# Second block's mixer: one written order of sixteen rounds for dilated attention and mLSTM, and six places for weights, in place of two generators taking turns

## The reference

```
def hybrid_mixer(h, w_in, gate_bias, g_q, g_k, g_mh, w_out):
    ...
    hm = bidirectional_mlstm(heads(mq, M_HEADS), heads(mk, M_HEADS) * (M_QK_DIM ** -0.5), heads(mv, M_HEADS),
                             gates[0], jax.nn.log_sigmoid(gates[1]), gates[2], jax.nn.log_sigmoid(gates[3]))
    hm = rms_norm(hm.transpose(0, 2, 1, 3), g_mh.reshape(M_HEADS, M_V_DIM))
    hm = (hm * jax.nn.sigmoid(mo.reshape(B, S, M_HEADS, M_V_DIM))).reshape(B, S, M_HEADS * M_V_DIM)
    ...
    ha = dilated_attention(qa, ka, heads(av, A_HEADS))
    ...
    return jnp.concatenate([hm, ha], axis=-1).astype(h.dtype) @ w_out
```

## Time and profile before

| what | value |
|---|---|
| median of 3 runs | 3207.26 us (3206.55 to 3207.32) |
| profiled execution | 3206.36 us, span 3204.4 us |
| PE busy | 3104.4 us (97% of the span) |
| DVE busy | 1905.7 us (59%) |
| ACT busy | 1042.2 us (33%) |
| POOL busy | 9.7 us |
| DMA | 369.19 MB, mean 115 GB/s |

### The profile page before, as it was taken

One profiled execution on the slowest core, in us unless ns is written; L12 is line 12 of the kernel. 1 busy time (PEld: TensorE's weight loads), 2 busy tenths in 40 slices (PEclk: granted clock), 3 DMA queues, 4 the chain that ended last, 5 costly groups with the idle time before them and its releaser, 6 DMA issues.

```text
span 3204.4 us, 37150 instructions
## 1 busy us (share of the span) xinstructions
PE 3104.4 (97%) x15012; PEld 2517.3 (79%) x15022; DVE 1905.7 (59%) x2786; ACT 1042.2 (33%) x1525; POOL 9.7 (0%) x23
## 2 busy tenths in 40 slices
PE   8999999998899999999999999999999998899998
PEld 7888888786678888788877888878887765578887
DVE  7876654636665555666657555466665565564434
ACT  4212222435442222422235222332223435442222
POOL 0000000000000000000000000000000000000000
PEclk9999999999999999999999999999999998899999
DMA  6433342210033443256532353235451220133231
GB/s 228 144 119 119 137 146 79 65 52 11 2 125 132 143 173 124 82 178 233 187 117 71 131 186 130 87 115 190 169 215 57 79 66 1 47 121 103 92 99 53
DMA packets 102964, 369.19 MB, mean 115 GB/s; under 512 B 11358, under 2 KB 12638, under 8 KB 102540
## 3 DMA queue, kind: packets, MB, share of 16 engines
q1 hardware_dynamic: 101788, 362.14, 33.2%
q0 software_dynamic: 1008, 4.69, 0.4%
HBM read 364.69 MB, written 2.10 MB: 114 GB/s over the span
## 4 chain that ended last, share of the span: by engine, by line
PE 86%; DVE 8%; ACT 4%; issue 1%; DMA 1%; SPq 0%; POOL 0%; DVEq 0%; ACTq 0%; POOLq 0%
PE ps L193 25%; PE ps L195 24%; PE ps L194 24%; PE ps L197 4%; PE ps L198 2%; DVE SQ L615 1%; DVE HL L604 1%; DVE WL L185 1%; PE ps L2869 1%; DVE XT L1038 1%; DVE RAW L1501 0%; DVE DUMP L306 0%; ACT WH L180 0%; DMA STG<-in_w_modt 0%; PE ps L500 0%
## 5 line engine op out<-in xcount | busy, mean ns | idle before, releaser
L193 PE MATMUL ps<-HH,WH 128*128 128x512 f32 x2400 | 947.2, 395 | 5.4 <-ACT S L915 2.2
L195 PE MATMUL ps<-HH,WL 128*128 128x512 f32 x2400 | 936.4, 390 | 0.0
L194 PE MATMUL ps<-HL,WH 128*128 128x512 f32 x2400 | 936.0, 390 | 0.0
L180 ACT ACTIVATE WH<-RAW 128x1024 fp32r<-128x1024 f32 x456 | 459.0, 1048 | 630.9 <-PE ps L195 361.8
L185 DVE TENSOR_TENSOR WL<-RAW,WH 128x1024 fp32r<-128x1024 f32 x456 | 542.7, 1219 | 75.3 <-ACT WH L180 75.1
L193 PEld LDWEIGHTS ps<-HH,WH 128*128 128x128 f32 x2400 | 450.9, 188 | 111.3 <-issue 10.2
L195 PEld LDWEIGHTS ps<-HH,WL 128*128 128x128 f32 x2400 | 450.9, 188 | 96.8
L194 PEld LDWEIGHTS ps<-HL,WH 128*128 128x128 f32 x2400 | 451.2, 188 | 95.7 <-issue 3.8
L1038 DVE SCALAR_TENSOR_TENSOR XT<-ps,DER,XT 128x512 f32<-128x512 f32 x512 | 346.6, 683 | 246.5 <-PE ps L195 231.7
L193 PE MATMUL ps<-GH,WH 128*128 128x512 f32 x1056 | 414.1, 392 | 4.8 <-DVE GL L946 4.8
L195 PE MATMUL ps<-GH,WL 128*128 128x512 f32 x1056 | 411.1, 389 | 0.0
(11 more groups left out here) (373 smaller groups left out, 2600.0 us busy)
## 6 DMA issues: line engine op xcount, KB each, us to landing
RAW<-in_w_modt SPq DMA_DIRECT2D x200, 512.0 KB, 5.0
RAW<-in_ffn_wi SPq DMA_DIRECT2D x182, 512.0 KB, 4.9
RAW<-in_w_gu SPq DMA_DIRECT2D x90, 512.0 KB, 4.5
RAW<-in_ffn_wo SPq DMA_DIRECT2D x88, 512.0 KB, 4.7
RAW<-in_w_in SPq DMA_DIRECT2D x44, 512.0 KB, 3.6
RAW<-in_w_down SPq DMA_DIRECT2D x44, 512.0 KB, 3.9
RAW<-in_w_out SPq DMA_DIRECT2D x16, 512.0 KB, 4.4
STG<-in_w_modt SPq DMA_DIRECT2D x10, 512.0 KB, 12.9
```

Source lines behind the costliest of these rows:

```text
L180: act.e.activation(u.hi, u.ld.view, ACT.Copy).then_inc(u.hi_done.sem, 1)
L193: pe.e.matmul(out, wh, x[0], start=first, stop=False)
L194: pe.e.matmul(out, wh, x[1], start=False, stop=False)
L195: m = pe.e.matmul(out, wl, x[0], start=False, stop=last)
```

## The change

`mlstm` and `dilated` are gone. One function, `rounds`, adds all their steps in one written order: for each r from 0 to 15 the attention pair r and the mLSTM unit r. `MlExp` is split into `MlWeights` (ScalarE) and `MlScore` (TensorE), so that they can stand apart. A has six places in place of four. `ptfree[3]` is not set any more, so all transposes go through bank 6. The weights of the output projection are split within the last steps.

```diff
-        self.afree = {s: NONE for s in range(4)}
+        self.afree = {s: NONE for s in range(6)}
...
-        self.A = sb("A", [128, 4, T])
+        self.A = sb("A", [128, 6, T])
...
-            s = m.na % 4
+            s = m.na % 6
...
-            self.side_by_side(self.mlstm(m, w, mix, a["w_out_2"]), self.dilated(w, mix))
+            self.rounds(m, w, mix, a["w_out_2"])
...
+        mixed = lambda k, ready: self.add(MixSplit(self, mix, [k], [ready]))
+        unit, last, den, quot, square, root, out = {}, {}, {}, {}, {}, {}, {}
+        split(0, True)
+        split(0, False)
+        self.add(MlMask(m, 0))
+        for r in range(16):
+            h, j = r // 4, r % 4
+            if r:
+                self.add(DilCount(w, r - 1))
+            unit[r] = self.add(MlWeights(m, h, j))
+            self.add(DilScore(w, r))
+            if r:
+                self.add(DilTrans(w, 2 * r - 2))
+            if h and j == 1:
+                quot[h - 1] = self.add(MlQuot(m, den[h - 1]))
+            self.add(MlScore(m, unit[r]))
+            if r:
+                self.add(DilTrans(w, 2 * r - 1))
+            if r == 1:
+                self.add(MlTurnFloor(m))
+            if h and j == 3:
+                out[h - 1] = self.add(MlOut(m, root[h - 1]))
+            if r > 1:
+                self.add(DilPV(w, r - 2))
+            if r:
+                last[r - 1] = self.add(MlSum(m, unit[r - 1]))
+            self.add(MlProd(m, unit[r]))
+            if h and j == 0:
+                den[h - 1] = self.add(MlDen(m, last[r - 1]))
+                self.add(DilDen(w, h - 1))
+            if h and j == 1:
+                square[h - 1] = self.add(MlSquare(m, quot[h - 1]))
+                self.add(DilQuot(w, h - 1))
+            if h and j == 2:
+                root[h - 1] = self.add(MlRoot(m, square[h - 1]))
+                mixed(3 + h, w.quot[h - 1].done)
+            if r in (2, 3):
+                split(1, r == 2)
+            if j == 3 and h < 3:
+                self.add(MlMask(m, h + 1))
+        self.add(DilCount(w, 15))
+        last[15] = self.add(MlSum(m, unit[15]))
+        self.add(DilTrans(w, 30))
+        den[3] = self.add(MlDen(m, last[15]))
+        self.add(DilTrans(w, 31))
+        self.add(DilPV(w, 14))
+        quot[3] = self.add(MlQuot(m, den[3]))
+        self.add(DilDen(w, 3))
+        self.add(DilPV(w, 15))
+        square[3] = self.add(MlSquare(m, quot[3]))
+        self.add(DilQuot(w, 3))
+        for k in range(2):
+            mixed(k, out[k].done)
+        root[3] = self.add(MlRoot(m, square[3]))
+        mixed(7, w.quot[3].done)
+        out[3] = self.add(MlOut(m, root[3]))
+        mixed(2, out[2].done)
+        mixed(3, out[3].done)
```

More of the change, by code:

```diff
@@ L2480, in vector @@
                                 m.MB[d * 4 + h].rearrange("p (n t) -> p n t", t=128), mk, ALU.add).then_inc(self.done[d].sem, 1)
-class MlExp(Step):
+class MlWeights(Step):
     def __init__(self, m, h, j):
@@ L2497, in __init__ @@
             self.off.append(m.P.s["ml_act"].next() if o.stop > o.start else self.diag[d])
-        self.qkfree = m.qkfree
-        self.qk = m.P.s["ml_mm"].next()
         m.unit[h, j] = self
@@ L2516, in scalar, with __init__ @@
                 act.e.activation(m.A[:, s, o], m.MB[d * 4 + h][:, o], ACT.Exp, bias=ub, scale=-1.0).then_inc(self.off[d].sem, 1)
+class MlScore(Step):
+    def __init__(self, m, x):
+        self.m, self.h, self.j = m, x.h, x.j
+        self.qkfree = m.qkfree
+        x.qk = m.P.s["ml_mm"].next()
+        self.done = x.qk
     def tensor(self, pe):
@@ L2527, in tensor @@
         pe.e.matmul(m.P.banks[0], m.KH[r, p, js], m.QL[r, p, :], start=False, stop=False)
-        pe.e.matmul(m.P.banks[0], m.KL[r, p, js], m.QH[r, p, :], start=False, stop=True).then_inc(self.qk.sem, 1)
+        pe.e.matmul(m.P.banks[0], m.KL[r, p, js], m.QH[r, p, :], start=False, stop=True).then_inc(self.done.sem, 1)
 class MlProd(Step):
@@ L3749, in mixer_hybrid, with rounds @@
         return [self.over]
-    def mlstm(self, m, w, mix, w_out):
+    def rounds(self, m, w, mix, w_out):
         m.qsplit, m.ksplit = {}, {}
[L3754 to L3759, removed]
-        self.add(MlFloor(m))
[L3761 to L3792, removed]
@@ new lines, in split @@
+        def split(p, query):
+            x, hi, lo, splits = (m.Q, m.QH, m.QL, m.qsplit) if query else (m.K, m.KH, m.KL, m.ksplit)
+            splits[p] = self.add(HiLo(self, x[:, p, :], hi[:, p, :], lo[:, p, :], []))
+        mixed = lambda k, ready: self.add(MixSplit(self, mix, [k], [ready]))
+        unit, last, den, quot, square, root, out = {}, {}, {}, {}, {}, {}, {}
+        split(0, True)
+        split(0, False)
+        self.add(MlFloor(m))
+        self.add(MlMask(m, 0))
[34 more added lines that the diff above has]
+                self.add(MlMask(m, h + 1))
@@ L3793, in mlstm @@
+        self.add(DilCount(w, 15))
+        last[15] = self.add(MlSum(m, unit[15]))
+        self.add(DilTrans(w, 30))
+        den[3] = self.add(MlDen(m, last[15]))
         self.new_ring()
         self.units = self.split([w_out[0]])
[L3795 to L3815, removed]
-                if q % 4 == 1:
-                    self.add(MixSplit(self, mix, [q // 4 + 3], [w.quot[q // 4 - 1].done]))
+        self.add(DilTrans(w, 31))
```

## The result

The change made the kernel slower by a little: the median of 20 runs is 3210.60 us, that of 20 runs of the kernel before 3205.51 us, a ratio of 1.0015 (95% interval 1.0008 to 1.0021), some 5 us. The profiled execution took 3211.23 us, with a span of 3209.4.

What follows compares the result with a forecast made beforehand. The order of the work, no engine filling the mixer stage, was the bound; 2661.3 + 100.2 + 12.35 = 2773.9 us starts the projection 9.4 us earlier, less 2.5 and 3.8 for the clock: gain 3.1, forecast 3204.2 us, range 3196 to 3212.

Steps and rivals of the forecast that it cites:

- The order's own rounds: Rounds of the three later heads: 7.45, 10.1, 7.6 and 8.2 us, 33.4 us a head, 100.2 us for three.
- The loop of 7.3 us: Ordinary round: score, maxima, exponentials, PT copy, second transposes, P·V and sums, each waiting for the one before, 7.3 us.
- MlDen's stall: First round of heads 1 to 3: MlDen waits for sums in VectorE's queue, making the next maxima 1.8 us late.
- The tail: From the end of unit 14's sums to the output projection's first product: 12.35 us.
- the 2.5 taken: Output projection's beginning: it starts at half clock after TensorE's idle stretches, costing 2.5 us (bounds 0 and 5.5).
- The start: First four rounds: masks and weights first make round 1 1.3 us later; round 4 starts at 2661.3, so no gain.
- The clock in the rounds: Round j=1 of three heads: a toss-up whether the clock falls, 3 x 0.5 x 2.5 = 3.8 us lost.
- Two of the signs that the prediction had named: Wrong if rounds without per-head work exceed 9 us; right if the projection starts between 2774 and 2780.
- The rival that the clock stays up: Clock stays up in rounds and tail, or VectorE stalls are shorter: gain 9.4 to 13 us, 3194 to 3200; chance 0.30.
- The slower rival: Clock falls at j=1 and stays down within the head, ordinary rounds grow to about 11 us: 3220; chance 0.08.
- The rival by which the change moves nothing: Same loop holds both orders; what the last 33 us give is paid by longer earlier rounds: 3204 to 3210; chance 0.19.
- The places: Six places for the weights instead of four cost and give nothing by themselves.

Runs made afterwards that it cites:

- the kernel with two tail edits: The change with sums, MlOut and start order moved, plus the weight split behind MlQuot and seven useless matmuls in the tail's waits: 3188.34 us, ratio 0.9944.

## Why the prediction was wrong, step by step

**The order's own rounds: right.** The loop of 7.3 us through banks 4 to 6 and the copy, MlDen's stall (1.8 us walked; the maxima stand 1.6 late in the trace, and moving MlDen gave 1.4), DilQuot's products and the lateness behind MlOut are all in the trace. With the wait filled the four rounds of a head are 7.5, 9.9, 7.6 and 7.8 us, against 7.45, 10.1, 7.6 and 8.2. VectorE kept its order, which was decisive: MlDen waited 5.06 us with counts and maxima behind it, and with MlDen moved the round shrank from 9.9 to 8.5. The Trainium skill (TensorE: Matmul & The Clock Gate, architectural detail) states this strict order of VectorE's queue, and the trace agrees.

**The tail: right**, 12.0 us for 12.35. Its cost in the projection's first blocks was smaller, 1.15 us (the first residual addition 6.95 us behind the first product, L1304 at 2792.24; 5.80 before, 2789.09 less 2783.29) for the 2.5 taken; the later fall in the projection cost 1.6 more, which the forecast's sum did not hold.

**The start: mis-sized.** I had the second score 1.3 us late and no loss by the fifth. The lateness is there, 1.2 us; the fifth score then came 31.7 us after the first instead of 29.2, with 17.1 us at half clock where it was 13.7 before. The larger part is round 1: walked at 7.9 to 8.5 us with "the same vector part", it took 9.6 (7.8 before), since at half clock TensorE alone fills it. The order of masks and exponentials has no part in that, for with it put back round 1 took 9.6 again; it took 7.8 in the kernel with two tail edits, whose clock came back at 2639.4, and 11.9 with five matmuls more.

**The clock in the rounds: the step that failed.** The prediction put it as a toss-up in one round of each head, 3 x 0.5 x 2.5 = 3.8 us, and gave the ordinary round's wait of 1.3 us no cost, noting only that it is less than the worst wait of the kernel before. The trace shows seven falls, three of them in the round that I named and four in the rounds on either side of it, which I had counted as free; the twelve rounds took 110.1 us against 100.2, so the term is 9.9 us in place of 3.8. Filling the waits brought 8 us back in spite of 20 us of added work on TensorE (16 x 1.27), and the traces with and without differ by 9 to 12 us in these rounds: the same size, shown a second way. What the estimate left out is that a wait of some 1.3 us stands in every one of sixteen rounds; of twelve rounds seven ran partly at half. The same wait, 1.2 to 1.5 us, brought no fall in rounds 7, 11, 12 and 14, so it makes a fall possible and not certain. The falls in round 4 (2668) and round 8 (2705) follow ordinary waits, with no stall of MlDen near. Two of the signs that the prediction had named came: round 4 took over 9 us with next to no work of a head in it (7.45 walked), and the projection started at 2785.3, not between 2774 and 2780.

So the walk's gain was real in the rounds and the tail, but only at full clock: with the waits filled they take 112.2 us, 10.1 less than before (the forecast's 9.4 for the whole stage). The half-clock rounds took all of that, and the start and the projection made the 5 us on top. Even filled, the kernel is only 2 us under the kernel before (3.7 by the two profiled executions), because the start loses 4.5 us there (33.5 for 28.9) and the projection's first blocks 1.6. The rival that the clock stays up came true only in the rounds of the kernels with filled waits. The slower rival had it right that several rounds of a head run slow and wrong that the clock stays down: it came back each time within 3 to 7 us, and a fall cost 1.4 to 2.9 us and not the 3.7 of a whole round, so its 3220 was too high. The rival by which the change moves nothing came nearest, with a range up to 3210, and for its reason: what the end gave was paid in longer rounds. That the measured 3210.60 lies inside the stated range of 3196 to 3212 is owed to the width of the range; the direction was wrong. The places gave nothing, as said.

The transpositions on TensorE over the stage, first in the change and then in the kernel with five matmuls a round; behind the last bar stands the idle time ahead of them, with what ended it.

```profile
L2847 PE MATMUL ps<-K,PP 128*128 128x128 f32 x128 | 22.8, 305 | 23.2 <-ACT PT L2854 19.5 <-DVE PP L2826 3.6
```

```profile
L2849 PE MATMUL ps<-K,PP 128*128 128x128 f32 x128 | 21.9, 297 | 7.2 <-DVE PP L2828 3.6 <-ACT PT L2856 3.4
```

The waits for the PT copy are the place to read: 19.5 us in the change, fifteen of them, one for each round and none longer than 1.6 by the view of waits; 3.4 us with the filling.

What stays open: which of the single falls comes in a given execution, and what decides between two equal waits. The falls lie at other rounds in most traces (the change with four places had them in the same seven), and the runs of a kernel spread over up to 13 us.

## What to carry to other kernels

A written order is judged by where TensorE waits in every round, not by the longest wait: a short wait that comes back each round costs its own time and, here, through the clock nearly as much again (9 to 12 us beside some 1.3 us in each of twelve rounds). Put the work that depends on nothing recent (here the sums of the unit before) into the place of that wait; this one move gave 16.6 us, more than three times what the whole reordering had cost. When a walk through the queues and the measured time part, add useless work into the wait: if the kernel gets faster, the clock is the likely difference, and the lengths of the same matmuls in the two traces settle it (1.98 and 1.09 us for P.V here). And when a new order is compared with an old one, ask how much of the old one's time ran at half clock: here the forecast set a stage measured with 51 us at half clock (0.17 of 151.3, doubled) against one walked almost wholly at full.

## What the runs showed of the hardware

Added matmuls can make a kernel faster: 80 of them, some 20 us of TensorE at full clock, took 8.3 us off. The clock fell to half behind waits of 1.2 to 1.6 us between work that came back every round, though not behind each of them; 32 matmuls (two a round, 0.5 us) were enough to stop the falls in the ordinary rounds of the traced execution. A matmul with 64 rows and 512 columns took 0.25 us from start to start when five of them repeated one product into one bank (1.27 us for five, 2668.16 to 2669.43).
